# Half-by-half evictions at the ends of matmul quarters, earlier roots, a bias row copied to DRAM first, and ten dummy matmuls

## The chip, the cores and the metric

One core of one Trainium2 chip runs the whole program. The time is the device time of one launch in microseconds (us); lower is better. TensorE is called PE here, VectorE DVE, ScalarE ACT, GpSimd POOL and SyncE SP, as in the profile.

## The reference

Two transformer blocks over 256 tokens of width 2048, in fp32. `rms` is a root-mean-square norm with a gain.

```
h = rms(x) @ w_in            -> attention q,k,v | recurrence q,f,i,g | two gates
y_attn  = sliding_window_attention(rotary(q), rotary(k), v, sinks)       # 16 heads of 64
y_hgrn  = rms(gated recurrence(q, f, i)) * silu(g)                       # 8 heads of 128
x += rms((sig(ga) * (y_attn @ w_attn) + sig(gb) * (y_hgrn @ w_hgrn)) @ w_out)
x += rms((silu(gate) * up) @ w_down)           # gate, up = rms(x) @ w_gate_up, width 5632
x += rms((p @ w_ple_proj) * sig(rms(x) @ w_ple_gate))
# second block
h = rms(x) @ w_in_2          -> sparse latent attention (top 64 keys, a bias row per head) | decay attention
x += mix @ w_o
x += conv_ffn(rms(x))        # width 5632, a convolution of 3 taps
return rms(x)
```

## The kernel before

**Tiles and ticks.** The weights (486 MB read) come as a stream of 512 KB units, eight 128x128 tiles each, into four buffers `raw`. Four tiles are a batch, and a batch is one *tick*; there are 1804. For every batch ACT casts the 128x512 of `raw` to fp32r as `hi` (`half`, L993), DVE writes the remainder as `lo` (`low_half`, L1482), and PE multiplies with both (L572), which with the split activations gives fp32 accuracy in three products. `hi` and `lo` have six slots, so the split of batch b waits until PE is done with batch b-6; ACT and DVE make the splits of tick t+5 (`LOOK`) in tick t.

**Two kinds of groups.** A *whole* group is 128 output features by 256 tokens in one bank. A *quarter* is 128 tokens by 512 output features in each of two banks, one for either half m of the tokens. In `batch_of_quarter` the last three batches (`SKEW`) are run for half 0 first and then, nine matmuls, for half 1; so half 0 of the quarter is complete about two microseconds ahead of half 1, and the batches' slots come free only with half 1.

**The order of work.** Every engine's program is written out by hand by tick: an `Agenda` holds generators that are due at a tick and `yield` the tick of their next piece. In tick t, ACT and DVE first make the split of t+5 and then run what is due; in a tick of the set `URGENT` what is due is run ahead of the split. Waits are on semaphores, in program order: an engine that waits holds back all that it has behind it.

**Block ends.** At three places (`ENDS`: "ffn" after `wout` 3 in ticks 416 to 431, "ple" after `down1` (3, 2) in 948 to 961, "mix2" after `proj` 3 in 1030 and 1031) a row-wise norm stands between two products. `carried` does it: squares of the last quarter on ACT (L1080), their sum (L1637), root (L1149) and reciprocal (L1641), the gained values (`gained`, L1482), the residual XT += Y * root in eight pieces `STEPS` (`make`, L1485, 128 to 384 features, two token halves each), transposes of 16 chunks on PE (`cross`, L603), and from each the split pair `XS` (`enter`: ACT L1259, DVE L1485). The next product needs chunk c in its tick c. `made_at`, `entered_at` and `CROSS` hold the ticks of pieces, entries and transposes. Between the block end and the next product lie two ticks of `proj` 0 ("ffn"), four of `proj` 1 and 2 ("ple"), or none ("mix2"). The four first groups of a product run abreast, tile by tile, but for the last `ALONE` = 3 tiles of each. The next norm's root by token is spread over the partitions by a matmul with `diag` (`next_root`, `spread_root`, due at `NORM_AT` + 2 on PE).

**First block's start.** The three quarters `qkv` (ticks 0 to 47) are turned with rotary by DVE (`quarter_of_heads`, L1485 and L1482, at ticks `TURN`) and transposed by PE (`turn`, L627, three ticks later). Eight attention steps follow, 18 ticks apart on two lanes: scores, softmax, transposes of the probabilities (L660) nine ticks after the scores.

**Bias rows.** Eight rows of 512 biases are made in `a_t5` (SBUF, one partition per head). POOL's queue writes each of them 128 times to a DRAM tensor (`t5rows`, 256 KB per head, L2254) at intervals of 12 ticks between 915 and 1040 us; the second block reads them back with a stride (L2236).

## Time and profile before

| | us |
|---|---|
| median of 3 runs (lowest to highest) | 2759.4 (2756.27 to 2760.2) |
| the profiled execution, its own time | 2753.84 |
| its span, first to last instruction | 2752.1 |
| PE busy / PE's weight loads | 2691.9 (98%) / 2285.4 (83%) |
| DVE busy | 1923.6 (70%) |
| ACT busy | 1541.0 (56%) |
| DMA queues, share of 16 engines | 55.7% + 3.1% |
| mean granted TensorE clock | 0.991 |

PE is busy for all but 60.2 us. Shares of busy time say little where PE waits for a chain of short instructions on the other engines; those places must be read by stretch and instruction by instruction. The granted clock is 1.00 at TensorE's 2.4 GHz and 0.50 at 1.2 GHz.

### The profile page before, as it was taken

How to read it: one execution, taken by the hardware profiler on the slowest of the kernel's cores; microseconds unless marked ns; L12 is line 12 of the kernel's file. 1: busy time of each engine (PE TensorE's matmuls, PEld its weight loads, DVE VectorE, ACT ScalarE, POOL GpSimd, SP SyncE). 2: the span in 40 equal slices, each digit the busy share in tenths (PEclk: the TensorE clock that was granted, in tenths of full speed). 3: DMA queues.
4: the chain of work that ended last, by engine and by line, in shares of the span. 5: the costliest groups of instructions: out<-in, count | busy, mean ns of one | idle time of the engine just before them, and what ended most of it. 6: DMA issues, size and time to landing. Idle time of an engine off the chain costs nothing.

```text
span 2752.1 us, 39728 instructions
## 1 busy us (share of the span) xinstructions
PE 2691.9 (98%) x14224; PEld 2285.4 (83%) x14224; DVE 1923.6 (70%) x3675; ACT 1541.0 (56%) x3037; POOL 17.0 (1%) x35
## 2 busy tenths in 40 slices
PE   8999999999999999999999999999999999999998
PEld 6778898888788888888887788887888888888886
DVE  6667777776677457756766678666678858876885
ACT  6565545555655445545556565545566646655664
POOL 0000000000000000000000000000000000000000
PEclk9999999999999999999999999999999999999999
DMA  7445455656566897666665554544656666666664
GB/s 255 130 137 153 153 159 156 223 186 221 162 196 188 176 199 206 186 196 185 191 192 160 176 151 153 172 145 129 200 163 196 188 190 192 190 190 192 186 191 154
DMA packets 136788, 493.20 MB, mean 179 GB/s; under 512 B 15680, under 2 KB 16192, under 8 KB 135824
## 3 DMA queue, kind: packets, MB, share of 16 engines
q1 hardware_dynamic: 134064, 480.11, 55.7%
q0 software_dynamic: 2240, 10.29, 3.1%
q8 instruction: 113, 1.85, 0.3%
q14 instruction: 83, 0.68, 0.1%
q10 hardware_dynamic: 288, 0.26, 0.0%
HBM read 486.41 MB, written 4.19 MB: 178 GB/s over the span
## 4 chain that ended last, share of the span: by engine, by line
PE 88%; DVE 4%; ACT 3%; DMA 3%; issue 1%; ACTq 0%; DVEq 0%
PE bank L572 87%; DMA raw<-in_ws_ffn 3%; DVE lo L1482 1%; ACT hi L993 1%; DVE X L1485 0%; DVE arena L1482 0%; PE bank L603 0%; DVE u_t L1482 0%; ACT sq_t L1080 0%; DVE arena L1485 0%; ACT arena L1327 0%; PE bank L660 0%; DVE arena L2067 0%; ACT L1327 0%; ACT arena L1043 0%
## 5 line engine op out<-in xcount | busy, mean ns | idle before, releaser
L1482 DVE TENSOR_TENSOR lo<-raw,hi 128x512 fp32r<-128x512 f32 x1804 | 1233.9, 690 | 776.9 <-ACT hi L993 694.1
L993 ACT CAST hi<-raw 128x512 fp32r<-128x512 f32 x1804 | 1106.8, 620 | 970.1 <-PE bank L572 888.5
L572 PE MATMUL bank<-XS,hi 128*128 128x512 f32 x4272 | 1181.3, 398 | 12.3 <-DVE XS L1485 5.8
L572 PEld LDWEIGHTS bank<-XS,hi 128*128 128x128 f32 x4272 | 732.7, 189 | 120.8 <-ACT hi L993 10.2
L572 PEld LDWEIGHTS bank<-XS,lo 128*128 128x128 f32 x4272 | 656.2, 189 | 91.9 <-DVE lo L1482 0.4
L572 PE MATMUL bank<-XS,lo 128*128 128x256 f32 x4272 | 681.2, 281 | 0.0
L572 PE MATMUL bank<-hi,HS 128*128 128x512 f32 x1696 | 473.7, 391 | 1.3 <-DVE u_t L1482 1.1
L572 PEld LDWEIGHTS bank<-hi,HS 128*128 128x128 f32 x1696 | 317.2, 188 | 67.5 <-issue 2.1
L572 PE MATMUL bank<-lo,HS 128*128 128x512 f32 x848 | 278.8, 390 | 0.0
L572 PE MATMUL bank<-hi,XS 128*128 128x512 f32 x960 | 274.8, 401 | 2.9 <-ACT hi L993 2.0
L572 PEld LDWEIGHTS bank<-hi,XS 128*128 128x128 f32 x960 | 179.8, 192 | 46.0 <-ACT hi L993 5.2
L572 PEld LDWEIGHTS bank<-lo,HS 128*128 128x128 f32 x848 | 159.6, 188 | 33.8 <-DVE lo L1482 0.4
L572 PE MATMUL bank<-lo,XS 128*128 128x512 f32 x480 | 157.5, 394 | 0.0
L572 PE MATMUL bank<-arena 128*128 128x128 f32 (+5 forms) x784 | 115.4, 296 | 1.3 <-ACT arena L1403 1.0
L999 ACT COPY tmp_t<-bank 128x256 f32<-128x256 f32 x307 | 111.7, 366 | 0.0
L1482 DVE TENSOR_TENSOR u_t<-bank,tmp_t 128x256 f32<-128x256 f32 x264 | 110.1, 418 | 0.1
L572 PEld LDWEIGHTS bank<-lo,XS 128*128 128x128 f32 x480 | 91.8, 191 | 20.0
L572 PEld LDWEIGHTS bank<-arena 128*128 128x128 f32 (+2 forms) x784 | 94.3, 185 | 12.3 <-issue 2.7
L1482 DVE TENSOR_TENSOR u_t<-u_t,r_t 128x256 f32<-128x256 f32 x224 | 95.3, 426 | 7.6
L1485 DVE SCALAR_TENSOR_TENSOR u_t<-u_t,prm 128x255 f32<-128x255 f32 (+1 forms) x176 | 85.0, 484 | 4.4
L1482 DVE TENSOR_TENSOR u_t<-u_t 128x256 f32<-128x256 f32 (+1 forms) x202 | 85.3, 422 | 4.0 <-ACT u_t L1060 1.0
L572 PE MATMUL bank<-HS,hi 128*128 128x512 f32 (+1 forms) x304 | 80.7, 386 | 4.5 <-DVE u_t L1482 4.5
(180 smaller groups left out, 1129.9 us busy)
## 6 DMA issues: line engine op xcount, KB each, us to landing
raw<-in_ws_ffn SPq DMA_DIRECT2D x528, 512.0 KB, 3.6
raw<-in_ws_mix SPq DMA_DIRECT2D x338, 512.0 KB, 3.6
raw<-in_ws_ple SPq DMA_DIRECT2D x35, 512.0 KB, 4.2
arena<-in_gains POOLq DMA_DIRECT2D x4, 1024.0 KB, 8.0
arena<-in_xt SPq DMA_DIRECT2D x8, 256.0 KB, 6.1
X<-in_xt POOLq DMA_DIRECT2D x1, 2048.0 KB, 10.5
t5rows<-arena POOLq DMA_DIRECT2D x8, 256.0 KB, 11.4
out<-arena SPq DMA_DIRECT2D x8, 256.0 KB, 2.9
```

What stands on the lines that cost most here:

```text
L572: return eng.matmul(o, l, r, start=start, stop=stop, skip_group_check=True)
L993: eng.copy(hi[:, b % SPL, :], raw[:, u % RAW, part * BW:(part + 1) * BW]).then_inc(halved.next(b), 1)
L999: eng.copy(low(g), bank[g.bank][:, T:2 * T]).then_inc(copied.next(g.g), 1)
L1482: return eng.tensor_tensor(o, a, b, op)
L1485: return eng.scalar_tensor_tensor(out=o, in0=a, scalar=s, in1=b, op0=op0, op1=op1)
```

## The change

- Block ends: `carried` starts one tick earlier and ahead of that tick's splits, and goes half by half: each half of the tokens has its own square, sum, root, reciprocal and residual pieces 0 and 1. `URGENT` now holds the last two ticks of every quarter. The residual pieces that fit are made in the ticks before the next product (`BEFORE`), and the first three chunks enter right behind.
- `ple` 3's sigmoids, and with them the load of the table with the root, are due one tick earlier on ACT and ahead of the splits; `proj` 0 and 1's copies are moved too.
- `ALONE` is 2. The root of the first norm is due two ticks earlier, of the others one tick (DVE).
- `qkv` 1 and 2 are turned by DVE in the quarter's last two ticks instead of the two after it. The attention's transposes and what follows them are due one tick later.
- Ten dummy 128x512 matmuls stand in PE's program ahead of the transposes of "mix2".
- The eight rows are copied to a DRAM tensor once, with a wait, and multiplied from there.
- The end of the program goes half by half; one of eight final scalings moves from ACT to DVE.

```diff
-ALONE = 3
+ALONE = 2
+BETWEEN = 10
+        ROOT_AT = {n: t - 1 for n, t in NORM_AT.items()} | {"mix": NORM_AT["mix"] - 3, "ple": E_PLE + 12}
+        BEFORE = {n: e - g.last - 1 for n, (_, g, e) in ENDS.items()}
         def made_at(name, s):
             _, g, e = ENDS[name]
-            between = e - g.last - 1
-            if s < 3:
-                return g.last
-            return g.last + s - 3 if s < 4 + bool(between) else e + STEPS[s][0] // P - 4
+            return g.last + s - 3 if s - 3 <= BEFORE[name] else e + STEPS[s][0] // P - 4
         def entered_at(name, c):
-            return g.last if c < 3 and e == g.last + 1 else CROSS[name][c]
+            return g.last + (name == "ple") if c < 3 else CROSS[name][c]
# PE
+            def idle(o, n):
+                for _ in range(n):
+                    mm(o, HS[:, 0, 0:P], HS[:, 0, :], True, True)
             def cross(name):
+                if name == "mix2":
+                    clear(2)
+                    idle(bank[2], BETWEEN)
...
-                    yield at + 9
+                    yield at + 10
                     on.wait_ge(a_dve, (x, "probs"))
...
-        URGENT = {plan.ticks - 1}
-        for n, (_, g, _) in ENDS.items():
-            URGENT |= {g.last, CROSS[n][0]}
+        URGENT = {g.last - k for g in plan.quarters for k in range(2)}
+        for n, (_, g, e) in ENDS.items():
+            URGENT |= {g.last - 1, g.last, g.last + 1}
# ACT, carried
-                root_by_token(n)
+                for m in range(2):
+                    (square_of_wout if name == "ffn" else square_of_down if name == "ple" else square_of_eout)(g, m)
+                    root_of_half(n, m)
...
-                    agenda.at(g.last, quarters[g.kind](g))
+                    agenda.at(g.last - (g is by["ple", 3]), quarters[g.kind](g))
# DVE, carried
-                sum_of_squares(n, after)
-                gained(g, k, 1, after)
-                root_by_token(n)
+                product(0)
+                gain(0)
+                sum_of_half(n, 0, (g.g, "square", 0) if name == "mix2" else (g.g, 0))
+                root_of_half(n, 0)
+                product(1)
+                make(0, 0)
+                make(1, 0)
+                sum_of_half(n, 1, (g.g, "square", 1) if name == "mix2" else (g.g, 1))
+                gain(1)
+                root_of_half(n, 1)
+                make(0, 1)
+                make(1, 1)
+                if BEFORE[name]:
+                    for m in range(2):
+                        make(2, m)
...
+            def root_of_half(n, m):
+                on.wait_ge(n_act, (n, "sqrt", m))
+                r = roots_of(n)[:, m:m + 1]
+                eng.reciprocal(r, r).then_inc(n_dve.next((n, "root", m)), 1)
+                on.wait_ge(n_dve, (n, "root", m))
...
-                yield 2
+                yield 2 if name == "mix" else 1
                 root_by_token(name)
...
-                    agenda.at(g.last, quarters[g.kind](g))
+                    agenda.at(g.last - (g.kind == "qkv" and g.i > 0), quarters[g.kind](g))
-                agenda.at(g.last, carried(name))
+                agenda.at(g.last - 1, carried(name))
-            agenda.at(plan.ticks, final())
+            agenda.at(plan.ticks - 2, final())
# POOL's queue
+            eng.dma_start(z_row, a_t5).then_inc(in_row.next(0), 16)
+            on.wait_ge(in_row, 0)
             for h in range(8):
                 on.wait_ge(rest, TABLE + 8 + 12 * h)
-                eng.dma_start(z[h:h + 1], a_t5[h:h + 1, :].unsqueeze(1).to_broadcast([1, P, 512])).then_inc(in_z.next(h), 16)
+                eng.dma_start(z[h:h + 1], z_row[h:h + 1, :].unsqueeze(1).to_broadcast([1, P, 512])).then_inc(in_z.next(h), 16)
```

## Rows read from the trace of the kernel before

**Rows 1.** The page: PE's share, and the splits on DVE and ACT.

```profile
PE 2691.9 (98%) x14224; PEld 2285.4 (83%) x14224; DVE 1923.6 (70%) x3675; ACT 1541.0 (56%) x3037; POOL 17.0 (1%) x35
L1482 DVE TENSOR_TENSOR lo<-raw,hi 128x512 fp32r<-128x512 f32 x1804 | 1233.9, 690 | 776.9 <-ACT hi L993 694.1
```

**Rows 2.** Busy time by stretch: us, busy by engine, granted clock, DMA share, GB/s.

```profile
0.00:220.00 220.00, 203.76 (x1017) 164.73 (x1017) 145.78 (x320) 137.98 (x309) 0.20 (x4) 0.95 0.53 172
430.00:460.00 30.00, 25.48 (x135) 20.97 (x134) 24.15 (x45) 18.92 (x37) 0.00 (x0) 1.00 0.35 106
700.00:750.00 50.00, 43.24 (x226) 36.38 (x225) 32.40 (x68) 30.77 (x71) 1.08 (x2) 0.93 0.51 162
938.00:1053.00 115.00, 110.83 (x560) 93.20 (x558) 59.04 (x106) 50.59 (x99) 3.14 (x6) 1.00 0.91 190
1460.00:1505.00 45.00, 40.81 (x183) 31.58 (x182) 31.52 (x65) 29.61 (x68) 0.00 (x0) 0.96 0.48 151
1560.00:1612.00 52.00, 44.66 (x232) 36.92 (x231) 34.99 (x72) 33.13 (x74) 0.00 (x0) 0.93 0.45 138
2040.00:2735.00 695.00, 695.00 (x3663) 596.62 (x3662) 543.08 (x995) 415.91 (x770) 0.00 (x0) 1.00 0.62 189
2735.00:2753.00 18.00, 6.32 (x28) 4.88 (x27) 4.49 (x10) 4.30 (x9) 0.00 (x0) 0.81 0.31 117
```

**Rows 3.** Timeline, 43 to 48 us: start, us, instruction, idle before and its releaser.

```profile
43.52 1.28 ACT L1149 ACT_TABLE_LOAD   x1 [0.54 <-DVE cols L1637]
...
47.05 1.23 PE L572 MATMUL bank<-arena,cst 128*128 128x128 f32 x4 [3.23 <-DVE arena L1489]
```

**Rows 4.** Timeline, 61 to 101 us: `qkv` 1 turned, and PE's transposes of it and of `qkv` 2.

```profile
61.47 1.53 DVE L1485 SCALAR_TENSOR_TENSOR arena<-bank,cols,arena 128x512 f32<-128x512 f32 x3
...
66.56 0.68 PE L627 MATMUL bank<-cst,arena 128*128 128x128 f32 x2 [2.27 <-DVE arena L1482]
...
100.44 0.45 PE L627 MATMUL bank<-cst,arena 128*128 128x128 f32 x2 [3.31 <-DVE arena L1482]
```

**Rows 5.** PE's waits, 60 to 220 us: us in total, times, longest.

```profile
PE bank L660 <- DVE arena L1482: 3.5, 4, 1.8
```

**Rows 6.** Timeline at the block end "ffn".

```profile
710.97 2.99 DVE L1485 SCALAR_TENSOR_TENSOR X<-arena,cols,X 128x128 f32<-128x128 f32 x8
...
717.10 2.04 PE L572 MATMUL bank<-XS,hi 128*128 128x512 f32 x4 [3.95 <-DVE XS L1485]
...
746.72 0.71 PE L572 MATMUL bank<-arena,cst 128*128 128x128 f32 x4 [0.97 <-DVE arena L1489]
```

**Rows 7.** Timeline at the block end "ple".

```profile
1480.48 0.48 DVE L1485 SCALAR_TENSOR_TENSOR XS<-bank,prm,XS 128x256 fp32r<-128x256 f32 x1
...
1482.33 1.17 PE L572 MATMUL bank<-hi,XS 128*128 128x512 f32 x4
```

**Rows 8.** Timeline at the block end "mix2".

```profile
1571.76 1.28 ACT L1084 ACT_TABLE_LOAD   x1
1571.80 0.68 DVE L1482 TENSOR_TENSOR arena<-arena,bank 128x512 f32<-128x512 f32 x1
...
1573.06 0.20 ACT L1084 ACTIVATE cols<-cst 128x2 f32<-128x2 f32 x1
...
1577.52 1.91 PE L603 MATMUL bank<-cst,X 128*128 128x128 f32 x6 [4.78 <-DVE X L1485]
```

**Rows 9.** Timeline at the start of the last product.

```profile
2019.49 0.68 PE L572 MATMUL bank<-arena,cst 128*128 128x128 f32 x4 [1.43 <-DVE arena L1489]
```

**Rows 10.** DMA issues: number, KB each, median us from issue to landing.

```profile
arena<-in_gains POOLq DMA_DIRECT2D x4, 1024.0 KB, 8.0
...
t5rows<-arena POOLq DMA_DIRECT2D x8, 256.0 KB, 11.4
```

**Rows 11.** Timeline of the end.

```profile
2735.72 1.07 PE L572 MATMUL bank<-hi,HS 128*128 128x512 f32 x4
...
2744.82 4.47 SPq L2323 DMA_DIRECT2D out<-arena  x8
```

More of the change, by code:

```diff
@@ L944, in tensor @@
             on.wait_ge(zeros, 0)
-            for _ in range(IDLE):
-                mm(bank[3], HS[:, 0, 0:P], HS[:, 0, :], True, True)
+            idle(bank[3], IDLE)
             for tick in range(plan.ticks):
@@ L1661, in quarter_of_down1 @@
                 q, p = g.i
-                if p == 0:
+                if p == 0 or g is by["down1", (3, 2)]:
                     return
                 for m in range(2):
-                    if m and g is not by["down1", (3, 2)]:
+                    if m:
                         yield 1
-                    before_ = by["down1", (q, p - 1)].g, m
-                    on.wait_ge(t_act if p == 1 else t_dve, before_)
-                    on.wait_ge(gemm, ("half", g.g, m))
-                    tt(Y[:, m, cut(q)], Y[:, m, cut(q)], bank[g.banks[m]], ALU.add).then_inc(t_dve.next((g.g, m)), 1)
-                    if m == 0 and g is by["down1", (3, 2)]:
-                        gained(g, 1, 0, (g.g, 0))
-                if p == 2 and q < 3:
+                    add_down(g, m)
+                if p == 2:
                     for m in range(2):
@@ L1676, in quarter_of_down1, with add_down @@
                         gained(g, 1, m, (g.g, m))
+            def add_down(g, m):
+                q, p = g.i
+                on.wait_ge(t_act if p == 1 else t_dve, (by["down1", (q, p - 1)].g, m))
+                on.wait_ge(gemm, ("half", g.g, m))
+                tt(Y[:, m, cut(q)], Y[:, m, cut(q)], bank[g.banks[m]], ALU.add).then_inc(t_dve.next((g.g, m)), 1)
             def quarter_of_ple(g):
@@ L1688, in quarter_of_ple, with last_product @@
                     gained(g, 2, m, (g.g, "square", m))
-            def quarter_of_proj(g):
-                if g.q < 3:
-                    return
-                for m in range(2):
-                    on.wait_ge(t_act, (by["ple", 3].g, m))
-                    on.wait_ge(gemm, ("half", g.g, m))
-                    tt(Y[:, m, cut(3)], gate_t[:, m, :], bank[g.banks[m]], ALU.mult).then_inc(t_dve.next((g.g, m)), 1)
-                    if m == 0:
-                        gained(g, 2, 0, (g.g, "square", 0))
-                yield
+            def last_product(g, m):
+                on.wait_ge(t_act, (by["ple", 3].g, m))
+                on.wait_ge(gemm, ("half", g.g, m))
+                tt(Y[:, m, cut(3)], gate_t[:, m, :], bank[g.banks[m]], ALU.mult).then_inc(t_dve.next((g.g, m)), 1)
             def quarter_of_x(g):
                 q = g.i if g.kind in ("o0", "o1") else g.i[0]
+                if g is by["down2", (3, 2)]:
+                    return
                 for m in range(2):
@@ L1719, in quarter_of_x, with add_to_x @@
                         with_final_gain(g, m)
+            def add_to_x(g, m):
+                q = g.i if g.kind in ("o0", "o1") else g.i[0]
+                if g.kind == "o1":
+                    on.wait_ge(t_dve, (by["o0", q].g, m))
+                elif g.kind == "down2":
+                    on.wait_ge(t_dve, (by["down2", (q, g.i[1] - 1)].g if g.i[1] else by["o1", q].g, m))
+                    on.wait_ge(crossed, ("ffn2", 4 * q + 3))
+                    for half in range(2):
+                        on.wait_ge(t_act, (by["o1", q].g, half))
+                on.wait_ge(gemm, ("half", g.g, m))
+                tt(XT[:, m, cut(q)], XT[:, m, cut(q)], bank[g.banks[m]], ALU.add).then_inc(t_dve.next((g.g, m)), 1)
             def with_final_gain(g, m):
@@ L1753, in carried, with product, gain, make @@
                 k = ("ffn", "ple", "mix2").index(name)
-                after = (g.g, "square", 1) if name == "mix2" else (g.g, 1)
-                sum_of_squares(n, after)
-                gained(g, k, 1, after)
-                root_by_token(n)
-                if name == "ffn":
-                    on.wait_ge(in_x2, 0)
-                def make(s):
+                def product(m):
+                    if name == "ple":
+                        add_down(g, m)
+                    elif name == "mix2":
+                        last_product(g, m)
+                def gain(m):
+                    gained(g, k, m, (g.g, "square", m) if name == "mix2" else (g.g, m))
+                def make(s, m):
                     a, b = STEPS[s]
@@ L1781, in carried @@
                         if parts_at[s] == tick:
-                            make(s)
+                            for m in range(2):
+                                make(s, m)
             def enter(name, c):
```

162 lines of the change are left out of this document (93 added, 69 removed).

## The prediction

> **What bounds the kernel now.** I read the page first: PE is busy 98% of the span, with 83% of weight loads beside it, while DVE and ACT have slack on the mean [rows 1]. Then the stretches: between 2040 and 2735 us PE is busy for 695.00 of 695.00 us [rows 2]; an edit there is worth nothing as long as it makes no wait. So the change can only touch what PE idles (60.2 us of the 2752.1) and what it loses where the granted clock is lower. The stretches put most of the idle time at few places: 16.2 us in 0 to 220, 4.5 in 430 to 460, 6.8, 4.2 and 7.3 at the three block ends, 4.2 in 938 to 1053, 11.7 after 2735 [rows 2]; some 4 more lie at the start of the last product. Last I read each of them in the timeline, for the instruction that PE waits for. In nearly all it is a short DVE instruction that stands behind splits or behind a chain of root steps [rows 3, 4, 6, 8, 9]. The cost of the clock: a batch's four matmuls with 512 columns take 2.04 us behind the wait at 717 [rows 6] and 1.07 at full speed [rows 11]; the mean of 0.95 over 0 to 220 is 22 us at the lower level (220 x 0.05 / 0.5), so up to 11 us of PE's time, and by the same sum (0.07 of 50, 0.04 of 45 and 0.07 of 52 us, over 0.5) the block ends have 18 us at half speed, in which PE is busy some three quarters of the time and loses half: 7 us.
>
> **The first 220 us.** (a) *First root.* PE waits 3.23 us for the spread of the root; a table load of 1.28 us stands in the chain [rows 3]. The sum now goes ahead of two splits and the root ahead of two, but the load stays, now behind a sum that can be ready at some 42.3 instead of 43.4; I take 1.3 us (0 if the last square is late, 3.2 at most). (b) *Turning `qkv` 1 and 2.* Each turn is 1.5 us plus an addition of 0.6 per half, behind splits [rows 4]. They now start as soon as the half is complete, two ticks earlier (a tick is six matmuls of 0.227, 1.4 us, with 0.227 from (1.07 - 0.39)/3 of [rows 11], 0.39 being a lone one), and the splits they pass have four ticks of slack. PE's waits of 2.27 (with 0.59 just before) and 3.31 us go: 2.9 + 3.3. (c) *Attention a tick later.* The four waits for probabilities, 3.5 us, longest 1.8 [rows 5], each shrink by a tick of 1.4: 3.1 go, 0.4 of the longest stays. ACT's and DVE's steps behind them move by the same tick, and the next head is 18 ticks on: no cost seen. Sum 10.6, bounds 5 and 13. (d) With fewer waits some stretches at half speed go. Of the up to 11 us I take 3.5, bounds 0 and 8, since not every wait is followed by one: the 4.5 us of waits in 430 to 460 have a clock of 1.00 [rows 2].
>
> **Block end "ffn".** Before, all hangs on half 1: its square ends near 710.1, then sum, gained values (0.68), root, reciprocal, and eight pieces in 2.99 us from 710.97 (0.27 for 128 features, 0.42 for 256), two splits, two more pieces, a split, entries; PE starts at 717.10 [rows 6]. In the change half 0's chain starts at 707.3, when its matmuls end (nine matmuls of 0.227 before 709.35). DVE's queue then reads: gain 708.8, sum, reciprocal 709.5, two pieces 710.2, second sum, gain 711.0, reciprocal, two pieces 711.8, piece 2 712.7, one split 713.3, entry 0 713.7. PE starts at about 713.8, 3.3 earlier. But the later work is only pushed: before chunk 3 come two entries, pieces 3, 4 and 5 (2.5 us; piece 5 was four ticks later) and five splits, so chunk 3 is in at 720.7 where PE wants it at 718.4: a new wait of 2.3. Before, PE came to that tick at 724.4 (717.10 and three ticks, one of them at half speed). Gain 3.7. `ALONE` = 2 lets chunks 14 and 15 come a tick later (a wait of 0.83 in the trace) and the root comes a tick earlier (0.97 [rows 6]), 1.8 in all, less 0.3 for a bank that is freed later. The new wait can bring the lower clock again: 0.7. Sum 4.5, bounds 0 and 8.
>
> **Block end "ple".** Four ticks lie between, so `made_at` now puts pieces 5, 6 and 7 (0.85, 0.85, 1.07 us) into ticks 963 to 965, which are urgent, ahead of the splits and of chunk 3; before, they were at 971 to 975. PE gets chunk 0 2.9 us earlier, but DVE's queue from piece 1's end at 1471.1 to chunk 3 holds 12 us of work (pieces 2 to 7 5.3, eight splits at 0.61 as they follow one another 4.9, four entries 1.7), and ends near 1483.2; before, it was 1480.96 and PE took it at 1482.33 [rows 7]. So PE is 0.9 later there, gets back two late waits for piece 7 and a cast (1.1), and has a wait of almost 4 us with the clock at risk (1.5). Sum -1.3, bounds -4 and +2.
>
> **Block end "mix2".** The sigmoids of `ple` 3 go ahead of a split on ACT, and the table load behind them does too: half(1034) now waits for the load to end, DVE's split of 1034 waits for that, and the product stands behind both. Half 1's sigmoid can't start before 1569.9, so the load runs to 1572.0, the cast to 1572.6, the split to 1573.3; the product that started at 1571.80 [rows 8] starts at 1573.3. Half by half, piece 0 is complete at 1578.6 against 1577.2, and PE starts 0.6 late. The ten dummies cost 10 x 0.227 = 2.3 us, all inside a wait of 4.78 us [rows 8]; if that wait were gone they would cost their 2.3. They shorten the idle time, which may keep the clock: worth 0 to 2.3. With `ALONE` and the root as above (1.8 - 0.3): sum 0.8, bounds -3 and +4.
>
> The row shows the table load taking 1.28 us, with the next instruction at 1573.06, 1.30 after its start [rows 8]. The Trainium skill (ScalarE: Activation LUTs, What ACT_TABLE_LOAD costs) counts some 2.66 us for a switch, a drain included; by that the product would be 1.4 us later still and this block end would lose 0.6. The row decides, and the sum keeps 0.8.
>
> **Start of the last product.** The root's wait of 1.43 us [rows 9] shrinks to 0.2 (root a tick earlier, its table load unchanged); an addition that now goes ahead of a split saves 0.7; a bank 0.8. Sum 2.7, bounds 0 and 3.5.
>
> **Bias rows.** Writing 256 KB from one partition takes 11.4 us, while 1024 KB read from one DRAM row takes 8.0 [rows 10]. In 938 to 1053 the DMA engines are busy 0.91 of the time for 190 GB/s, in 2040 to 2735 0.62 for 189 [rows 2]: the writes hold the engines, `raw` comes late, PE waits for casts 4.2 us. From DRAM I expect 2.5 to 4 us per row, which four `raw` buffers cover: gain 4.0. The copy of the rows with its wait stands only before POOL's own queue, some 10 us ahead of the first use. Bounds: 0 (a row still takes 11.4, now through DRAM) and 4.2.
>
> The Trainium skill (SBUF — State Buffer, Door 1: The DMA port swizzle) lets one port give 27 GB/s: an estimate of 9.7 us for 256 KB, to which the row's 11.4 is close. The Trainium skill's fixed 2 us and 436 GB/s (same page, The DMA setup-cost knee) would give an estimate of 2.6 us once no single port is read; no trace so far shows that.
>
> **The end.** Eight stores are issued in 4.47 us from 2744.82 [rows 11], and the last lands 2.8 after it. The first store can go at 2743.2, behind half 0's scaling; the issues then set the end: gain 1.6, bounds 0.5 and 2. Splits, quarters and evictions elsewhere: 0, under PE's unbroken 695 us.
>
> **Sum.** 10.6 + 3.5 + 4.5 - 1.3 + 0.8 + 2.7 + 4.0 + 1.6 = 26.4 us: 2753.84 becomes 2727.4. The median of the runs shown is 5.6 above that execution; on its scale 2759.4 - 26.4 = 2733.
>
> **Rivals.** *Block ends give nothing back* (chance 0.25): DVE's queue is as long as before, and what goes forward is taken back at chunk 3, with half speed after each new wait. For it: DVE is the releaser in [rows 6], and my own sums for "ple" and "mix2"; against: "ffn" gains even with the push. The three give -5 instead of +4: 2742. *The clock comes back too* (0.15): with the waits most half-speed stretches go, 5 us more early and 4 more at block ends: 2724. For it: the low means stand where the waits are; against: 430 to 460. *It doesn't do what it says* (0.05): earlier places in the queues wait for the same semaphores and only rows and end pay, 5.6 us, with 2 from the roots: 2752. *Slower* (0.04): each row written from DRAM reads one 2 KB row 128 times and takes longer than 11.4 us, say 16; then 8 x 4.6 = 36.8 us fall on PE beside the present 4.2, against 22.4 gained elsewhere: 2774. It turns slower from 11.4 + 22.4/8 = 14.2 us per row. The 8.0 us for four times the bytes speaks against.
>
> **Numbers.** Forecast 0.51: 2733. Anything within 0.2% (5.5 us) counts as no change, which is about what a measurement tells. Faster 0.51 + 0.25 + 0.15 + 0.03 = 0.94; same 0.02; slower 0.04. The range, 2720 to 2748, leaves out the last two rivals and the sum of all upper bounds.
>
> **What would show it.** Right: no PE wait over 1 us on L627 and L660; t5rows landing under 5 us and a DMA share near 0.65 in that stretch; PE at 713.8 or so after "ffn" and then a wait near 2 us for XS at its fourth tick; after "ple" one of 3 to 4 us there; at "mix2" the product later than before relative to the last matmul. Wrong: waits of the old size at L627, a row over 11 us, or new waits behind quarters in the stretches that were unbroken.

## The result

The kernel with the change takes 2717.8 us (median of 4 executions, 2712.8 to 2720.9) against 2757.8 (4 executions, 2755.6 to 2760.2) of the kernel before on the same chip: a ratio of 0.985, 95% interval 0.983 to 0.987. That is about 40 us less. The forecast was 26 us less (2733), and its range ended at 2720; the measured time lies 2 us below it. The sign was right, the size too small by a third.

### The profile page after: what moved, and what is told of

Its sections match the earlier page's. It is cut to its first block, busy times and chain, and to the rows that moved or that the text cites. A ratio compares the mean times of both kernels' runs of the same rounds, so it can differ in the third digit from the quotient of the medians.

```text
span 2719.1 us, 39768 instructions
## 1 busy us (share of the span) xinstructions
PE 2681.9 (99%) x14234; PEld 2280.7 (84%) x14234; DVE 1924.8 (71%) x3684; ACT 1547.1 (57%) x3040; POOL 17.5 (1%) x36
## 4 chain that ended last, share of the span: by engine, by line
PE 94%; DVE 3%; DMA 1%; ACT 1%; issue 1%; SPq 0%; DVEq 0%; ACTq 0%
PE bank L576 93%; DMA raw<-in_ws_mix 1%; DVE lo L1516 1%; ACT hi L1004 0%; DVE X L1519 0%; PE bank L615 0%; ACT sq_t L1091 0%; DVE arena L1516 0%; DVE arena L1519 0%; DVE XS L1519 0%; DVE arena L2149 0%; PE bank L672 0%; DVE u_t L1516 0%; ACT arena L1429 0%; PE bank L799 0%
```

## The profile after

The profiled execution of the changed kernel took 2720.91 us, the slowest of its four, with a span of 2719.1; that of before took 2753.84 and was faster than all its others. The two profiles differ by 33 us. First the page: the share of the engines, and the queue on which the bias rows travel.

```profile
PE 2681.9 (99%) x14234; PEld 2280.7 (84%) x14234; DVE 1924.8 (71%) x3684; ACT 1547.1 (57%) x3040; POOL 17.5 (1%) x36
...
q0 software_dynamic: 2272, 10.31, 1.2%
```

Beside [rows 1], PE is busy 10.0 us less (2691.9 to 2681.9), although it has ten more matmuls, the dummies, which take 2.4. So its real work became 12.4 us shorter with not one matmul less, which can only be its speed, or waits hidden within what counts as busy (the ends of matmuls are modelled). It idles 37.2 us instead of 60.2; without the dummies' 2.4, 20.6 of waiting are gone. 20.6 and 12.4 make the 33.

Next the stretches that answer to [rows 2], each moved to where the same work now lies (us, busy by engine PE, PEld, DVE, ACT, POOL, granted clock, DMA share, GB/s).

```profile
0.00:220.00 220.00, 212.01 (x1124) 173.89 (x1125) 158.62 (x344) 147.47 (x328) 0.20 (x4) 1.00 0.58 187
411.00:441.00 30.00, 25.51 (x137) 21.04 (x137) 23.64 (x44) 18.97 (x37) 0.00 (x0) 1.00 0.35 105
682.00:732.00 50.00, 46.74 (x259) 39.75 (x258) 37.15 (x82) 34.45 (x80) 1.08 (x2) 1.00 0.56 172
910.00:1025.00 115.00, 115.00 (x587) 98.02 (x586) 68.64 (x118) 60.24 (x110) 3.14 (x6) 1.00 0.70 208
1430.00:1475.00 45.00, 41.03 (x184) 31.73 (x183) 31.52 (x66) 29.82 (x68) 0.00 (x0) 0.96 0.46 151
1532.00:1584.00 52.00, 47.16 (x244) 39.54 (x243) 36.16 (x79) 34.07 (x76) 0.00 (x0) 0.93 0.46 138
2011.00:2700.00 689.00, 689.00 (x3635) 591.57 (x3634) 538.28 (x988) 413.51 (x764) 0.00 (x0) 1.00 0.63 190
2700.00:2720.00 20.00, 9.86 (x44) 7.84 (x42) 7.19 (x16) 5.23 (x11) 0.00 (x0) 0.81 0.28 105
```

The mean clock of the first 220 us went from 0.95 to 1.00: PE now runs at 2.4 GHz through all of it. The same happened at "ffn" (0.93 to 1.00), but not at "ple" (0.96) and "mix2" (0.93). In the stretch of the bias rows PE doesn't idle any more, and the DMA engines are busy for 0.70 of it instead of 0.91. The waits of 430 to 460, now at 411 to 441, are untouched, as is the unbroken last product.

Then the timeline, for the places of [rows 3, 4, 6, 7, 8, 9, 11]. On L639, which was L627, no wait of over 1.00 us is left, and no wait for probabilities [rows 5] at all.

```profile
44.54 1.28 ACT L1177 ACT_TABLE_LOAD   x1
...
48.01 0.71 PE L576 MATMUL bank<-arena,cst 128*128 128x128 f32 x4 [2.80 <-DVE arena L1523]
...
94.22 0.66 PE L639 MATMUL bank<-cst,arena 128*128 128x128 f32 x4 [1.00 <-ACT arena L1039]
...
695.18 1.16 PE L576 MATMUL bank<-XS,hi 128*128 128x512 f32 x4 [0.93 <-DVE XS L1519]
701.75 1.16 PE L576 MATMUL bank<-XS,hi 128*128 128x512 f32 x4 [1.46 <-DVE XS L1519]
...
1452.15 1.33 PE L576 MATMUL bank<-hi,XS 128*128 128x512 f32 x4 [3.22 <-DVE XS L1519]
...
1540.93 1.28 ACT L1095 ACT_TABLE_LOAD   x1
...
1542.34 0.61 ACT L1004 CAST hi<-raw 128x512 fp32r<-128x512 f32 x1
...
1542.75 2.43 PE L576 MATMUL bank<-HS 128*128 128x512 f32 x10
...
1543.59 0.68 DVE L1516 TENSOR_TENSOR arena<-arena,bank 128x512 f32<-128x512 f32 x1
...
1549.13 1.54 PE L615 MATMUL bank<-cst,X 128*128 128x128 f32 x6 [3.95 <-DVE X L1519]
...
1988.25 0.68 PE L576 MATMUL bank<-arena,cst 128*128 128x128 f32 x4 [0.32 <-DVE arena L1523]
...
2711.89 4.47 SPq L2407 DMA_DIRECT2D out<-arena  x8
```

The reader should see the new waits at the fourth chunk of a block: 1.46 us at "ffn" (701.75) and 3.22 at "ple" (1452.15). Both were forecast (2.3, and almost 4). At "mix2" the chain reads as forecast: table load, cast, and the product behind them at 1543.59. The last matmul before the dummies ends at 1542.75, so the product starts 0.84 us after it; before, it started 0.94 ahead of it. Last the DMA issues that answer to [rows 10]: with the row read from DRAM, 256 KB land in 5.3 us instead of 11.4.

```profile
t5rows<-t5row POOLq DMA_DIRECT2D x8, 256.0 KB, 5.3
```

To see where the time came from, I set the start of the n-th split of the weight stream (`lo` on DVE) in one trace against the same split of the other; this is what "by the splits" means below. The difference grows like this (us gained at each step, forecast beside it):

```
                                 measured   forecast
first 220 us                       18.5       14.1   (waits 10.6, clock 3.5)
block end "ffn"                     5.6        4.5
bias rows                           5.8        4.0
block end "ple"                     0.0       -1.3
block end "mix2"                    0.0        0.8
1200 to 1980 us                    -0.9        0
start of the last product           2.5        2.7
end of the program                  1.5        1.6
sum                                33.0       26.4
```

## The experiments

The theory: what the forecast said of waits holds, and the missing time is PE's clock. The stretches at 1.2 GHz (dips from here on) follow PE's waits, and go with them. One dip doesn't fit, in either kernel (first before, then after):

```profile
1840.00:1860.00 20.00, 20.00 (x78) 14.08 (x77) 9.60 (x24) 5.85 (x12) 0.00 (x0) 0.91 0.34 107
```

```profile
1810.00:1830.00 20.00, 20.00 (x73) 14.30 (x72) 9.19 (x23) 4.59 (x9) 0.00 (x0) 0.83 0.36 105
```

PE is busy for all of the 20 us there, for a good part with matmuls of 128 and 256 columns, and the clock falls all the same. The profiles of ends alone, late pieces and `best1` don't have this dip, all others do; no experiment here says what brings it.

The rivals: the waits gave more than the rows showed (they hide within busy time, or are longer in executions that weren't profiled); or the parts help each other, so that none alone gives its share.

For both I also use what each execution lists: its span and its mean granted clock. Span times clock is what the span would be if each stretch at the lower level had passed at full speed; the remainder is the clock's share, an upper bound, since it counts idle time too. The clock is listed to 0.001 (2.8 us), so only means over several executions tell something, and a mean over four is still uncertain by 1 to 2 us.

```
kernel            executions  mean span  share of clock   rest
before                59       2754.4        23.1        2731.3
changed                4       2715.6        10.2        2705.4
changed, again         4       2714.7        10.2        2704.5
start alone            4       2735.8        16.4        2719.4
turns alone            7       2746.6        19.6        2727.0
turns filled          10       2748.2        15.9        2732.3
attention later       10       2747.8        21.7        2726.1
first root alone      11       2750.6        20.5        2730.1
rows alone            10       2745.9        21.1        2724.8
ends alone             4       2742.2        19.2        2723.0
no dummies             4       2714.2        10.9        2703.4
late pieces            4       2708.8         5.4        2703.4
table load later       4       2712.4         8.1        2704.3
best1                  4       2709.3         6.8        2702.6
best2                  5       2706.7         5.4        2701.3
```

### The first 220 us

**Start alone** (`start_alone`): kernel before with the edits of the first root, the turns and attention.

```
+ agenda.at(... - (3 if name == "mix" else 1), next_root(name))
+ agenda.at(g.last - (g.kind == "qkv" and g.i > 0), quarters[g.kind](g))
+ URGENT |= {g.last - k for g in plan.quarters if g.kind == "qkv" for k in range(2)}
- yield at + 9
+ yield at + 10
...
```

Expected:

> The kernel before with the edits of the first 220 us alone: the first root two ticks earlier, qkv 1 and 2 turned in their quarter's last two ticks and ahead of splits, attention a tick later. Theory A (the parts add, and most of the miss is the clock of this stretch): split 200 is made 18 us earlier than before, 9 from waits and 9 to 10 from the granted clock, which stays at 1.00 from 0 to 220; whole kernel 18 us faster. Theory B (part of it came from the rest of the change): 10 to 14 us, as I had summed it.

Measured: 2738.1 us against 2756.2, ratio 0.9933 (0.9919 to 0.9948), 18 us less. By the splits 21.0 us are gained within the first 220 us, and the mean clock there is 1.00, with the rest of the kernel as it was. So this gain doesn't need the other parts. In the table of executions 11.9 us of it lie outside the clock and 6.7 in it.

**Turns alone** (`turn_alone`): only the edit of the turns, with the last two ticks of the `qkv` quarters urgent.

```
+ agenda.at(g.last - (g.kind == "qkv" and g.i > 0), quarters[g.kind](g))
+ if g.i == 0: yield TURN[0] + m - g.last
+ elif m: yield 1
+ URGENT |= {g.last - k for g in plan.quarters if g.kind == "qkv" for k in range(2)}
...
```

Expected:

> The kernel before with only the turning of qkv 1 and 2 moved ahead. Theory A: the waits of 2.9 and 3.3 us go, and with them the two half-speed stretches behind them (66 to 70 and 101 to 104 us, 1.7 us of work each): 9 to 10 us faster; the stretches at 46 and 162 us stay. Theory B (the lower clock comes from the light matmuls of attention and the transposes, not from waits): 6 us faster, all four stretches stay.

Measured: 2747.6 against 2756.2, ratio 0.9969 (0.9958 to 0.9980), 8.7 us less; 10.8 by the splits. The waits of 2.27 (with 0.59 before it) and 3.31 us become none and 1.95, now for a copy of ScalarE; so 4.2 of the 10.8 are waits at the turns themselves. Some 1.5 were there by split 30, from the first weights coming in earlier in this execution, which is no part of the edit. The other 5.1 are the clock in the stretches below: 0.11 of 15 us and 0.17 of 20. The stretches of both kernels (us from:to, columns as above), first of before:

```profile
40.00:60.00 20.00, 16.77 (x66) 13.44 (x66) 11.33 (x27) 12.37 (x24) 0.00 (x0) 0.83 0.50 158
60.00:75.00 15.00, 12.14 (x51) 9.32 (x50) 9.61 (x20) 4.72 (x9) 0.00 (x0) 0.89 0.43 140
95.00:110.00 15.00, 11.69 (x61) 9.79 (x59) 10.91 (x27) 8.34 (x22) 0.00 (x0) 0.89 0.30 101
155.00:175.00 20.00, 18.23 (x77) 13.83 (x76) 10.84 (x24) 12.40 (x32) 0.00 (x0) 0.83 0.42 127
```

and of the turns alone:

```profile
60.00:75.00 15.00, 15.00 (x72) 12.13 (x71) 10.67 (x24) 6.92 (x15) 0.00 (x0) 1.00 0.51 172
95.00:110.00 15.00, 14.22 (x79) 12.09 (x80) 10.45 (x25) 9.82 (x20) 0.00 (x0) 0.89 0.44 137
155.00:175.00 20.00, 19.84 (x99) 15.32 (x98) 11.48 (x24) 11.03 (x25) 0.00 (x0) 1.00 0.54 159
```

In the first of them PE issues 72 matmuls instead of 51 in the same 15 us: the wait went (12.14 to 15.00 busy) and the clock came up. In the second, where a wait of 1.95 us is left, the clock still has its dip. In the third the clock is at 1.00 although attention's wait of 1.77 us ahead of it is still there: of that more below.

**Turns filled** (`turn_filled`): the kernel before, with dummy matmuls where PE stands still at the turns. No step of another engine starts earlier.

```
+ if g.i and k == 0:
+     for _ in range(9 + 2 * g.i):
+         mm(bank[b], XS[:, 15, 0:P], XS[:, 15, :], True, True)
```

Expected:

> The kernel before, with 11 and 13 dummy matmuls in PE's program ahead of the transposes of qkv 1 and 2, so that the two waits are filled but not shortened (the dummies' results are overwritten). Theory A (the clock falls because PE stands still): same instants of turning, no half-speed stretch at 66 and 101 us, 3 to 3.5 us faster. Theory B (it falls for another reason): no gain, or 0.5 us slower.

This is the experiment that separates the clock from the waits. The dummies in its timeline, and its stretches:

```profile
62.22 2.66 PE L572 MATMUL bank<-XS 128*128 128x512 f32 x11
...
94.24 3.12 PE L572 MATMUL bank<-XS 128*128 128x512 f32 x13
```

```profile
60.00:75.00 15.00, 14.45 (x69) 11.46 (x68) 9.34 (x17) 5.07 (x9) 0.00 (x0) 1.00 0.50 169
95.00:110.00 15.00, 14.64 (x84) 12.31 (x83) 11.05 (x24) 9.53 (x24) 0.00 (x0) 1.00 0.36 109
155.00:175.00 20.00, 18.23 (x76) 14.13 (x76) 11.91 (x29) 11.13 (x24) 0.00 (x0) 0.83 0.44 133
```

PE does 5.8 us of useless work, and the kernel is faster: 2749.2 against 2756.2, ratio 0.9980 (0.9971 to 0.9989), 5.5 us by the ratio, 7 by the medians, more than the 3 to 3.5 expected; by the splits 4.0 in the first 220 us. (The profiled execution, 2754.83, was the second longest of its ten.) Both dips at the turns are gone; the one behind attention's wait of 1.77 us, which the edit doesn't touch, stays. In the table of executions all of the gain is in the clock's share (23.1 to 15.9) and none in the rest (2731.3, 2732.3). So these dips come from PE standing still. In the profile the two are worth 0.11 of 15 us each, 3.3 in all, about half of the 6.2 us of waits ahead of them; over the executions the clock gains 7.2, about as much as those waits. Why it gains more there than in the profile isn't shown.

**Attention a tick later** (`attention_later`): only those lines, on the kernel before.

```
- yield at + 9
+ yield at + 10
- yield at + 12
+ yield at + 13
...
```

Expected:

> The kernel before with PE's, ACT's and DVE's steps of attention one tick later, nothing else. By the prediction 3.1 us from the four waits for probabilities. By the theory that half-speed stretches follow such waits, the one at 162 to 169 us goes too (6.8 us at half speed, up to 3.4 us more), and those at 46, 66 and 100 stay: 5 to 6.5 us in all by split 200. Rival 'waits only': 3.1. Rival 'it adds up otherwise': the whole of the first 220 us gained 18.5 to 21 with turns alone 10.8, so 8 to 10 here would mean that attention and not the root holds the rest.

Measured: 2749.4 against 2754.1, ratio 0.9980 (0.9971 to 0.9989), 5.5 us less by the ratio; 6.9 by the splits, of which all but 1 come between 147 and 224 us of before's time. The dip there is gone. But at the turn of `qkv` 2, which the edit doesn't touch, PE now waits 3.91 us instead of 3.31, and the dip behind that wait is longer, 0.77 over 95 to 110 us instead of 0.89:

```profile
95.00:110.00 15.00, 11.30 (x58) 9.43 (x58) 8.82 (x22) 8.15 (x21) 0.00 (x0) 0.77 0.20 70
155.00:175.00 20.00, 20.00 (x100) 15.76 (x99) 15.74 (x34) 14.47 (x32) 0.00 (x0) 1.00 0.49 160
```

Over the ten executions the kernel has 5.2 us less outside the clock and only 1.4 less in it, which can't be told from none. So the gain of this part is the waits; that its dip is gone in the profile is not seen in the mean clock.

**First root alone** (`root_alone`), only the sum, root and spread of "mix" two ticks earlier.

```
- agenda.at(NORM_AT.get(name, E_PLE + 13) - 1, next_root(name))
+ agenda.at(NORM_AT.get(name, E_PLE + 13) - (3 if name == "mix" else 1), next_root(name))
...
```

Expected:

> The kernel before with the first root's sum, root and spread as in the changed kernel, nothing else. Theory 'the three parts add up': 3.3 to 4.6 us by split 200 (what is left of 21.0 to 22.3 beside turns 10.8 and attention 6.9), of which 1.3 to 1.9 from the wait (3.23 falls to 1.3 to 1.9) and the rest from the half-speed stretch at 46 to 53 us becoming shorter or going. Rival 'only together': 1.3 to 1.9 us here with the half-speed stretch in place, and the rest of the 21 needs the other two edits. Rival 'the root gives nothing' (the last square is late): within 0.5 us.

Measured: 2753.6 against 2756.9, ratio 0.9985 (0.9976 to 0.9994), 3.3 us by the medians and 4.1 by the ratio, as by the first theory. In its profile the wait is 0.90 us instead of 3.23. The table load is just as long; the sum and the load start 3.0 and 3.3 us earlier than in before (40.32 and 40.22), PE comes to that point 1.0 earlier:

```profile
43.69 0.71 PE L572 MATMUL bank<-arena,cst 128*128 128x128 f32 x4 [0.90 <-DVE arena L1489]
```

```profile
40.00:60.00 20.00, 16.91 (x77) 13.05 (x75) 15.72 (x39) 12.31 (x23) 0.00 (x0) 1.00 0.62 189
95.00:110.00 15.00, 15.00 (x96) 12.76 (x94) 10.77 (x25) 9.82 (x20) 0.00 (x0) 1.00 0.46 140
```

Its splits gain 10.6 us in this one execution. Some 1.6 were there by split 30, from the first weights coming in earlier, and the last row shows the clock at 1.00 just behind a wait of 3.31 us that this kernel still has (it ends at 94.60). In before and in ends alone the same wait is followed by a dip. Attention's wait of 1.77 us is another case: a dip follows it in before and in turns filled, none in turns alone and in this kernel. So a wait makes a dip likely and not certain, and one profile of one kernel is not enough to price one. Over 11 executions the root is worth the 3 to 4, of which 1.2 lie outside the clock and 2.6 in it.

By the ratios the three give 4.1 + 8.5 + 5.5 = 18.1 us, and the start as a whole 18.5. The parts add up, within their intervals (2.5 to 3.0 us either way for a part, 4.0 for the whole); they don't need each other.

### The bias rows

**Rows alone** (`dma_alone`): only the row written to DRAM and multiplied from there.

```
+ eng.dma_start(z_row, a_t5).then_inc(in_row.next(0), 16)
+ on.wait_ge(in_row, 0)
- eng.dma_start(z[h:h + 1], a_t5[h:h + 1, :]. ...)
+ eng.dma_start(z[h:h + 1], z_row[h:h + 1, :]. ...)
```

Expected:

> The kernel before with the bias rows copied to DRAM once and multiplied from there, nothing else. Profiles of both kernels show the row writes falling from 11.4 to 5.3 us. Theory A (the writes held up the weight fetches, and with them PE): PE's waits for casts between 938 and 1053 us (4.2 us) go, 4 to 6 us faster in all, all four early half-speed stretches stay. Theory B (the rows cost nothing and the stretch gained from what came before it): within 1 us of before.

Measured: 2748.0 against 2756.2, ratio 0.9969 (0.9959 to 0.9978), 8.5 us less. In its profile:

```profile
925.00:1040.00 115.00, 115.00 (x575) 97.60 (x574) 67.30 (x112) 60.68 (x109) 3.67 (x7) 1.00 0.69 204
```

```profile
t5rows<-t5row POOLq DMA_DIRECT2D x8, 256.0 KB, 5.2
```

By the splits it gains 5.8 us where [rows 2] shows 4.2 of idle time. The waits of before, 760 to 1460 us, for TensorE's weight loads (us in total, times, longest), explain that:

```profile
PEld bank L572 <- ACT hi L993: 5.4, 5, 2.4
...
PEld bank L572 <- DVE lo L1482: 0.4, 1, 0.4
```

The loads stood 5.4 + 0.4 us for casts and splits, and PE's matmuls, whose ends are modelled, hide a part of that in their own busy time. In rows alone these waits are gone. That still isn't 8.5. The delays differ between executions, and the profile of before has short ones: in the profile of turns filled, with the same slow rows, PE's waits in this stretch are 5.7 us instead of 4.2, and its splits lose 3.5 there. All six other profiles with slow rows lose against before's in this stretch, 1.6 to 3.5 us, 2.4 in the mean. With the 5.8 that makes 8.2. In the table of executions rows alone has 6.5 us less outside the clock and 2 less in it.

### The block ends

**Ends alone** (`ends_alone`): the changed kernel without its edits to the start and the rows, and without the urgent ticks of the `qkv` and `hi` quarters.

```
- ROOT_AT = ... | {"mix": NORM_AT["mix"] - 3, "ple": E_PLE + 12}
+ ROOT_AT = ... | {"ple": E_PLE + 12}
- agenda.at(g.last - (g.kind == "qkv" and g.i > 0), quarters[g.kind](g))
+ agenda.at(g.last, quarters[g.kind](g))
- yield at + 10
+ yield at + 9
...
```

Expected:

> Only the block ends, the roots of ffn, ple, mix2, ffn2, the dummies and the program's end are as changed; turns, attention, first root and bias rows are as before. From the ledger of the whole change I expect about +5.5 us by the end of block end 'ffn', 0 at 'ple', 0 at 'mix2', +2.5 at the start of the last product, +1.5 at the end: 9 to 10 us less than before (2746 to 2748). Rival 'the ends owe their gain to the early start' (DVE with more slack, a clock already high): then under 5 us here, and the change's parts don't add up. Rival 'block ends give nothing back': the wait at 'ffn' chunk 3 and half-speed stretches take it all, under 3 us. What the trace must show: half-speed stretches of the first 220 us all there (46, 66, 100, 162), the one at 'ffn' gone.

Measured: 2745.1 against 2757.8, ratio 0.9951 (0.9937 to 0.9966): 13.5 us less by the ratio, more than the 9 to 10 expected, though the interval reaches down to 9.4. By the splits: "ffn" 5.7, "ple" 1.5, "mix2" 0.3, start of the last product 2.9. The rival, that this gain needs the start, is out. With the 18.5 of the start and the 8.5 of the rows it makes 40.5, the whole change.

**No dummies** (`no_dummies`), in the changed kernel:

```
- BETWEEN = 10
+ BETWEEN = 0
```

Expected:

> The changed kernel without the ten dummy matmuls at 'mix2' (BETWEEN = 0). Theory 'they keep nothing': the half-speed stretch at 'mix2' is there with them (1548.6 to 1555.4) and without; the wait for piece 0 grows from 3.95 to 6.2 us by the 2.3 us they filled, and the time is that of the changed kernel within 1 us. Rival 'they keep the clock up part of the way': without them the half-speed stretch comes a window earlier or is longer, and the kernel is 1.5 to 3.5 us slower than the changed one. Rival 'they cost': 2 us faster without, if they stand in the way of the transposes.

Measured: 2716.2, ratio to before 0.9850 (0.9835 to 0.9865), the same as the changed kernel (0.9853). The wait grows as it should:

```profile
1547.87 1.54 PE L615 MATMUL bank<-cst,X 128*128 128x128 f32 x6 [6.21 <-DVE X L1519]
```

Its clock over 1540 to 1560 us is 0.74, and 0.83 in the changed kernel: 0.09 of 20 us, 1.8 at most, much of it where PE stands anyway. By the splits the block end is 0.2 us worse. With 4 us of standing still left, ten dummies buy next to nothing. The stretches, of no dummies and of the changed kernel:

```profile
1540.00:1560.00 20.00, 13.47 (x62) 10.94 (x60) 13.85 (x32) 11.78 (x27) 0.00 (x0) 0.74 0.35 105
```

```profile
1540.00:1560.00 20.00, 15.73 (x71) 12.90 (x70) 13.00 (x30) 12.23 (x27) 0.00 (x0) 0.83 0.31 98
```

**Pieces 5 to 7 late again** (`late_pieces`): as in the kernel before, they are made just ahead of their own chunks, and not right behind the block end.

```
- return g.last + s - 3 if s - 3 <= BEFORE[name] else e + STEPS[s][0] // P - 4
+ return g.last + s - 3 if s - 3 <= min(BEFORE[name], 1) else e + STEPS[s][0] // P - 4
```

Expected:

> The changed kernel with pieces 5, 6, 7 of 'ple' and 5 of 'ffn' made where they were made before, so that DVE's queue ahead of chunk 3 is 2.8 us shorter at 'ple' and 0.85 at 'ffn'. Theory (the backlog of pieces makes the wait of 3.22 us at chunk 3 of 'ple', with half speed behind it): the wait falls under 0.8 us, the half-speed stretch at 1453 goes too, and the block end gains 2 to 4 us; the whole 2714 to 2716. Rival 'the splits make it': the wait stays above 2 us, no gain. Rival 'late pieces come late': waits for pieces 6 and 7 of about 1 us in all come back as before and eat the gain.

Measured: 2710.5, ratio 0.9830 (0.9816 to 0.9845). That is below the 2714 to 2716 expected. On the same chip the two other versions of the changed kernel took 2716.2 and 2714.1; the changed kernel itself didn't run beside it. The wait of 3.22 us at "ple" has become

```profile
1447.91 1.17 PE L576 MATMUL bank<-hi,XS 128*128 128x512 f32 x4 [0.58 <-DVE XS L1519]
```

and the clock of this block end is 1.00 instead of 0.96:

```profile
1430.00:1475.00 45.00, 42.83 (x199) 33.33 (x198) 33.90 (x71) 33.79 (x76) 0.00 (x0) 1.00 0.49 155
```

By the splits "ple" now gains 3.4 us against before, where the changed kernel gains none, and the wait of 1.46 at "ffn" is gone too. So the three urgent pieces were the backlog, as the forecast of "ple" had it, and the wait cost its dip as well. Most of the gain over the executions is in the clock's share (5.4 against 10.2 for the changed kernel).

**Table load later** (`table_later`): ScalarE loads its table two ticks later, behind the cast for which the split and the product wait.

```
+ yield 2
  root_table()
```

Expected:

> The changed kernel with ScalarE's table load at the end of 'ple' 3 moved two ticks on, behind the cast of the split that the product stands behind. Theory (the load of 1.28 us stands between sigmoid and cast, and the cast, its split and the product behind it make piece 0 late): the product starts 1.3 us earlier, PE's wait for piece 0 falls from 3.95 to 2.7 us, 1.2 us faster. Rival: the load now stands ahead of the first square of half 0 and delays the root by as much: 0. Rival: the shorter wait also saves the half-speed stretch of 6.8 us: 3 to 4 us faster.

Measured: 2714.1, ratio 0.9843 (0.9827 to 0.9860): too close to the changed kernel's 0.985 to tell by the time. The timeline tells it:

```profile
1537.88 1.28 ACT L1095 ACT_TABLE_LOAD   x1
...
1538.51 0.68 DVE L1517 TENSOR_TENSOR arena<-arena,bank 128x512 f32<-128x512 f32 x1
...
1539.19 2.43 PE L576 MATMUL bank<-HS 128*128 128x512 f32 x10
...
1544.09 1.54 PE L615 MATMUL bank<-cst,X 128*128 128x128 f32 x6 [2.48 <-DVE X L1520]
```

The product starts 0.68 us ahead of the dummies instead of 0.84 behind, and the wait falls from 3.95 to 2.48, all of the 1.5 the load had cost.

### Both kernels bettered

**The changed kernel again, and two built from it** (`after_again`, `best1`, `best2`). `best1` is late pieces and late table load together; `best2` is that with

```
- BETWEEN = 10
+ BETWEEN = 20
```

Expected:

> The changed kernel once more, beside two kernels built from it: 2713 to 2720 us, ratio to before between 0.983 and 0.987. If its profile has fewer half-speed stretches than the first one's four (7 + 3 + 7 + 9 us long), its own time is shorter by about half of what is missing; that would show that some 7 us between the ledger of the first pair of profiles (33.0) and the medians (40) are the executions' own spread and no part of the change.

> Late pieces and late table load together. They act at two different block ends, 'ple' and 'mix2', so they should add up: 5.0 + 1.2 (with no more than a half-speed stretch of 3.4 us, 1.7 us of time, either way) = 6 to 8 us less than the changed kernel: 2708 to 2711. Rival: an earlier start of 'mix2' runs into something else and only one of the two counts: 2711 to 2714.

> best1 with 20 instead of 10 dummy matmuls ahead of the transposes of 'mix2'. They take 4.5 us instead of 2.3 in a wait that is then 2.5 us, so PE stands still for some 0.3 us there and starts no later. Theory (standing still is what the half-speed stretch at 'mix2' follows): the stretch of 3.4 us behind it goes, worth 1.7 us against best1. Rival (the reason is not the standing still, since ten dummies kept nothing): no difference to best1 within 1 us. Rival: the dummies end late by a few 0.1 us and cost.

Measured on one chip, against 2754.1 of before: the changed kernel again 2716.1, ratio 0.9860 (0.9847 to 0.9874); `best1` 2711.4, ratio 0.9841 (0.9827 to 0.9854), 4.8 us less than the changed kernel beside it, somewhat under the 6 to 8 expected; `best2` 2708.3, ratio 0.9832 (0.9818 to 0.9845), 7.8 less. The profile of the changed kernel again has as many dips before the last matmul as the first and took 2716.5, by the splits with 3.8 us more gained in the first 220 us. They are all there by split 30: the first weights came in earlier, and PE waited 1.28 us for the root, not 2.80. That is how much one part of the start varies between executions of one kernel.

In `best2` PE stands still for 0.21 us at "mix2", behind the twenty dummies:

```profile
1535.17 4.69 PE L576 MATMUL bank<-HS 128*128 128x512 f32 x20
...
1540.08 1.06 PE L615 MATMUL bank<-cst,X 128*128 128x128 f32 x6 [0.21 <-DVE X L1520]
```

```profile
1532.00:1584.00 52.00, 50.67 (x285) 42.84 (x283) 42.86 (x95) 38.65 (x83) 0.00 (x0) 1.00 0.46 143
```

The clock of that block end is 1.00. But it is 1.00 in the profile of `best1` too, the fastest of its four executions, and by the splits they gain 3.7 and 3.8 us there against before, where the changed kernel gains none. The medians differ by 3.0, and the slowest execution of `best2` (2709.83) is as fast as the fastest of `best1` (2709.84). That the dummies keep the clock up in those executions of `best1` that weren't profiled fits this and the table above (5.4 against 6.8), but no profile shows it: it stays open.

## Why the prediction was wrong in size

**The clock, term (d): this is the step that failed.** I gave 3.5 us to "some stretches at half speed go", reasoning that not every wait is followed by one, since the four in 430 to 460 aren't. And I charged the block ends 0.7 and 1.5 for dips that might come. The net of the clock in my sum was 1.3 us. Measured over the executions, its share fell by 12.9 us (23.1 to 10.2); the rest fell by 25.9 (2731.3 to 2705.4), and the terms of my sum other than the clock make 25.1. So nearly all of the miss is the clock: 6.7 us of its share went with the start alone, 3.9 with the ends alone, 2.0 with the rows alone. By the profiles: in the first 220 us 18.5 us are gained; what PE idles there fell by 8.3 (16.24 to 7.99) and the remaining 10.2 are speed, against 3.5. All four dips of the start are gone, and turns filled shows for the two at the turns that this comes from the standing still alone. The example that I let speak against was a poor one: it says that a wait need not bring a dip, and nothing of the dips that the trace did have, all but the one at 1840 to 1860 us with a wait in front of it. The right sum was at hand: the mean of 0.95 gives up to 11 us for the start, and if the waits ahead of its dips go, up to all of it comes back. It was my rival "the clock comes back too", to which I gave 0.15 and 2724.

That the terms outside the clock agree as a sum is partly luck: by the executions the start gave 11.9 against 10.6, the rows 6.5 against 4.0, and the block ends with the end of the program 8.3 against 10.5.

**First root (a), 1.3 forecast.** Worth 3 to 4 alone, the wait and the dip behind it. Of the wait of 3.23 us 0.90 is left there, and 2.80 and 1.28 in the two profiles of the changed kernel; so the wait gives 0.4 to 2.3, by execution. The bound of 3.2 left out the clock.

**Turns (b), 2.9 + 3.3.** The first wait went wholly; the second keeps 1.00 us (1.95 alone), now for ScalarE's copy into the arena, which I hadn't looked at as the next in line. It gave 2.3, not 3.3.

**Attention (c), 3.1.** Right on the waits: none of the 3.5 us is left. Alone it gained 5.2 us outside the clock, more than these waits; where the rest of it lies isn't shown.

**"ffn".** Forecast 4.5, measured 5.6. Chunk 0 starts 0.93 us behind the last matmul instead of 3.95, 3.0 earlier against 3.3 forecast; the new wait is at the fourth chunk, 1.46 against 2.3; no dip came where I had charged 0.7, and the old one went. The mean clock of the stretch rose from 0.93 to 1.00.

**"ple".** The backlog is as I said: 3.22 us against "almost 4", with the clock at 0.96. The late waits for piece 7 and a cast went too, and the sum is 0.0 against -1.3. Late pieces shows that the mechanism was read rightly.

**"mix2".** 0.0 against 0.8. The product is 1.8 us later against the last matmul (1.5 forecast) and PE's transposes 1.6 (0.6 forecast): they start 6.4 us behind it (2.43 of dummies, 3.95 of waiting), before 4.78. The 1.5 from the chunks and the root pay for this. The dummies cost nothing and saved nothing that could be told.

The table load takes 1.28 us in the row, as in [rows 8], and moved away it gave back 1.5 of the wait. The Trainium skill (ScalarE: Activation LUTs, What ACT_TABLE_LOAD costs) counts 2.66 us for a switch, the load and a drain together; this trace shows no drain, the next instruction on ScalarE starts 1.30 us after the load's start.

**Bias rows.** 4.0 forecast with 4.2 as the upper end; 5.8 in the profile, 8.5 in the comparison of medians. The upper end was no bound: it counted what PE idled, and PE's weight loads waited 5.8; and it took the profiled execution for the typical one, which loses 2.4 more there. A row lands in 5.3 us, outside the 2.5 to 4 I expected, for which no row stood; the four buffers cover it just as well; the DMA share of 0.70 is near the 0.65 named.

**Last product and end.** 2.5 and 1.5 against 2.7 and 1.6. The root's wait fell to 0.32, and the tail behind the last matmul from 10.8 to 9.2 us.

**The scale.** I took 26.4 from the median of before as it stood, 5.6 us above its profiled execution. Those 5.6 were no fixed part of the kernel: the mean span of 59 executions lies only 2.3 above the profiled one, and 2.4 us of longer delays in the bias rows, which the change removes, are as much. So 33 us between the profiles are 40 between the medians: outside the clock the profiled execution of before was some 4 us better than its mean (2752.1 x 0.991 = 2727.3 against 2731.3), and the one of after some 3 worse (2708.2 against 2705.4), both to within the 1.4 us by which a listed clock is rounded.

With 12.9 for the clock in place of 1.3 my sum gives 38.0, and the mean spans differ by 38.8; against the median of before that is 2721.

## What to carry to other kernels

Price a wait of TensorE with the stretch at the lower clock behind it: in a row by stretch it counts as busy time, so it doesn't look like part of the wait, and here it was worth half as much again over all executions (12.9 against 25.9 us). The price is one to expect and no certainty: the same wait had a dip behind it in one kernel and none in another, and one dip had no wait in front of it. Where a necessary wait remains, cheap matmuls that fill it almost wholly gain time; a filling that leaves 4 us of it gains next to nothing. What is put ahead of its need on an engine's queue goes to somebody else's expense: the pieces and the table load that the change moved forward each made the wait behind them, and moved back they gave some 5 us. And the profile of one execution bounds a delay by DMA from neither side; the weight loads' waits, not PE's idle time, are the view for it.

## What was not expected of the hardware

- The same wait of 3.31 us is followed by a granted clock of 0.89 over 95 to 110 us in before and of 1.00 in the profile of the first root alone; the waits of 430 to 460 us, 4.5 in all, brought a dip in none of the profiles.
- The granted clock is 0.91 over 1840 to 1860 us of before and 0.83 over 1810 to 1830 us of after, with PE busy for all of both stretches.
- Writing 256 KB to DRAM takes 11.4 us from one partition of SBUF and 5.3 from a row in DRAM; the share of the DMA engines over the stretch falls from 0.91 to 0.70 while they move more, 208 GB/s instead of 190.
- 5.8 us of useless matmuls, put where PE would have stood still, made the kernel 5.5 us faster.
